# The output blocks of the last attention head, placed over all seven of its visits instead of the last six

## The reference

```
h = modulate(rms_norm(x, mix_norm), sh2, sc2)
q, f_fwd, f_bwd, i, g, rx, rgate = split(h @ w_in)
o_hg = hgrn2_mixer(q, f_fwd, f_bwd, i, g, ...)   # 4 heads x 128, chunkwise, both directions
       # per head: scores with decay between all pairs of tokens, o = scores @ v,
       # o = rms_norm(o) * silu(g)
o_rg = rglru_mixer(rx, rgate, ...)               # gated linear recurrence, 4 tiles of 128 channels
y = concat([o_hg, o_rg]) @ w_out                 # 1024 x 1024
x = x + g2 * y
```

## Time and profile before

| | us |
|---|---|
| median of 3 runs | 1004.42 |
| lowest and highest run | 1002.71, 1004.58 |
| the profiled execution, its own time | 1005.18 |
| its span in the profile | 1003.5 |
| TensorE (PE) busy in the span | 978.0 (97%) |
| VectorE (DVE) busy | 790.5 (79%) |
| ScalarE (ACT) busy | 511.7 (51%) |

### The profile page before, as it was taken

The page is one execution under the profiler, slowest core; times in us unless marked ns, Lnnn a source line. Parts: engine busy times, 40 slices in busy tenths (PEclk is TensorE's granted clock), DMA queues, the critical chain, the costliest instruction groups (busy, mean ns, idle before and its releaser), DMA issues.

```text
span 1003.5 us, 18868 instructions
## 1 busy us (share of the span) xinstructions
PE 978.0 (97%) x6956; PEld 851.7 (85%) x6956; DVE 790.5 (79%) x1052; ACT 511.7 (51%) x700; POOL 234.6 (23%) x229
## 2 busy tenths in 40 slices
PE   7999999999999999999999989999999999999997
PEld 6779999999888888686677767788999999988887
DVE  6788899988788858879999985878888999673334
ACT  6545444455333133688977963575554454433311
POOL 0025554452112301101100000402554454100100
PEclk9999999999999999999999999999999999999999
DMA  9568888884788826622222202245888787552322
GB/s 350 222 179 203 199 187 200 183 201 151 261 294 284 310 94 230 198 95 79 66 84 63 66 22 79 70 126 140 207 209 199 178 198 168 189 189 85 104 84 85
DMA packets 65622, 163.79 MB, mean 163 GB/s; under 512 B 6848, under 2 KB 9168, under 8 KB 65568
## 3 DMA queue, kind: packets, MB, share of 16 engines
q1 hardware_dynamic: 45296, 110.80, 32.9%
q0 software_dynamic: 18992, 50.16, 21.7%
q10 hardware_dynamic: 1280, 2.10, 0.9%
HBM read 158.83 MB, written 2.10 MB: 160 GB/s over the span
## 4 chain that ended last, share of the span: by engine, by line
PE 83%; DVE 7%; ACT 5%; issue 2%; DMA 1%; SPq 1%; DVEq 0%; ACTq 0%
PE psum L2030 14%; PE psum L2032 13%; PE psum L2031 13%; PE psum L2119 11%; PE psum L2121 11%; PE psum L2120 11%; DMA early<-wada 1%; PE psum L2427 1%; DVE wlo L1209 1%; ACT whi L640 1%; PE psum L2421 1%; DVE forms L1549 1%; PE psum L2351 1%; PE psum L2352 1%; PE psum L2353 1%
## 5 line engine op out<-in xcount | busy, mean ns | idle before, releaser
L1209 DVE TENSOR_TENSOR wlo<-raw,whi 128x1024 fp32r<-128x1024 f32 x94 | 119.4, 1270 | 110.9 <-ACT whi L640 110.5
L640 ACT ACTIVATE whi<-raw 128x1024 fp32r<-128x1024 f32 x92 | 97.3, 1058 | 207.0 <-PE psum L2032 193.0
L2030 PE MATMUL psum<-ghi,whi 128*128 128x512 f32 (+2 forms) x384 | 143.4, 373 | 0.0
L2031 PE MATMUL psum<-glo,whi 128*128 128x512 f32 (+2 forms) x384 | 142.6, 371 | 0.0
L2032 PE MATMUL psum<-ghi,wlo 128*128 128x512 f32 (+2 forms) x384 | 142.6, 371 | 0.0
L2030 PE MATMUL psum<-hhi,whi 128*128 128x512 f32 x304 | 122.5, 403 | 1.9 <-DVE wlo L1209 1.9
L2119 PE MATMUL psum<-forms,hi 128*128 128x256 f32 x432 | 119.2, 276 | 0.0
L2120 PE MATMUL psum<-forms,hi 128*128 128x256 f32 x432 | 119.2, 276 | 0.0
L2121 PE MATMUL psum<-forms,lo 128*128 128x256 f32 x432 | 119.2, 276 | 0.0
L2032 PE MATMUL psum<-hhi,wlo 128*128 128x512 f32 x304 | 118.7, 390 | 0.0
L2031 PE MATMUL psum<-hlo,whi 128*128 128x512 f32 x304 | 118.6, 390 | 0.0
(11 more groups left out here) (299 smaller groups left out, 2428.2 us busy)
## 6 DMA issues: line engine op xcount, KB each, us to landing
raw<-wu SPq DMA_DIRECT2D x96, 512.0 KB, 3.4
ada<-wada POOLq DMA_DIRECT2D x56, 512.0 KB, 5.0
sraw_a<-ws SPq DMA_DIRECT2D x36, 256.0 KB, 4.0
sraw_a<-ws SPq DMA_DIRECT2D x18, 512.0 KB, 4.0
sraw_b<-ws SPq DMA_DIRECT2D x36, 256.0 KB, 3.1
sraw_a<-ws POOLq DMA_DIRECT2D x36, 256.0 KB, 4.2
raw<-ws SPq DMA_DIRECT2D x36, 256.0 KB, 3.9
raw<-ws SPq DMA_DIRECT2D x18, 512.0 KB, 4.0
```

The costliest lines, as they stand in the source:

```text
L640: nc.scalar.activation(whi[:, slot, :], raw[:, slot, :], ACT.Copy).then_inc(hi_done, 1)
L1209: nc.vector.tensor_tensor(wlo[:, slot, :], raw[:, slot, :], whi[:, slot, :], ALU.subtract).then_inc(lo_done, 1)
L2030: nc.tensor.matmul(dst, a, rhi, start=start, stop=False)
L2031: nc.tensor.matmul(dst, a, rlo, start=False, stop=False)
```

## The change

Before, the first visit of the last head had no output blocks in front of it, and visits 1 to 6 had four each. After, a table gives the first block of each visit: four blocks stand in front of visits 0, 1 and 2, and three in front of visits 3 to 6. The sum is 24 both ways.

```diff
@@ -368,6 +368,8 @@
+
+        OUT_AT = (0, 4, 8, 12, 15, 18, 21, 24)
@@ -2492,8 +2494,8 @@
                 for g, steps in enumerate(STEPS_AT[r == 3]):
                     if r < 3:
                         z_half(first + g // 2, g % 2)
-                    elif g:
-                        out_blocks(4 * (g - 1), 4 * g)
+                    else:
+                        out_blocks(OUT_AT[g], OUT_AT[g + 1])
                     if (r, g) in ((1, 0), (2, 0), (3, 0)):
                         pv(r - 1)
                     for s in steps:
```

## The result

The change made the kernel slower, by more than the range allowed: 1015.07 us median of four runs (1012.29 to 1017.14), against 1003.92 for the kernel before in the same comparison (1002.71 to 1004.58). The ratio is 1.0106, with a 95% interval of 1.0085 to 1.0128. The forecast was 1011.2, the range 1009.0 to 1014.2.

The account below looks back on a forecast made before the run. PE, busy 97%, was taken as the bound, with DVE pacing the last head from score step 2. Step 2 6.9 us late left step 10 6.8 us late: 1004.42 + 6.8 = 1011.2 us, range 1009.0 to 1014.2.

Parts of the forecast that it names:

- The mechanism of the waits: Last head: PE waits 6.9 us at block 0, then 1.3, 1.1 and 1.9 us at later visits.
- the clock: Last head: half clock for 3.6 us from block 0's restart; the old half clock around step 0 gone.
- Part 1: Blocks 0 to 3 ahead of pv(2): PE idles 6.9 us for ylo of tile 0; score step 2 6.9 us late.
- Rival (d): Seam: ylo of tile 0 already there, blocks fill the gap, step 2 1.5 us early: 1002.9 us; chance 0.03.
- Part 2: Blocks 8 to 11 ahead of step 3: PE waits 1.3 us more for ylo of tile 2, covered by step 6.
- Part 3: Three blocks before visits 3 to 6: 1.9 us idle before block 16; step 10 6.7 to 6.9 us late.
- rival (b): Steps 2 to 10: DVE's chain has slack, time given back: +2.3 us, 1006.7; chance 0.10 with halfway cases.
- I take half clock at the restart and for 3.6 us: At block 0 after 6.9 us idle: 8.4 of 12 matmuls at half clock, four blocks take 4.4 us.
- Rival (a): Blocks 16 to 20: a second clock drop, 3.4 us at 1.2 GHz costing 1.7 us: +8.5, 1012.9; chance 0.28.
- rival (c): Seam: half clock through blocks 0 to 3 and pv(2), 4.1 us more: +10.9, 1015.3; chance 0.05.

Follow-up runs that it names:

- b3: The kernel before, profiled again without an edit: 1005.03 us.
- b1: The kernel before, profiled again without an edit: 1003.93 us.
- b2: The kernel before, profiled again without an edit: 1002.42 us.
- e11: The kernel before with filler matmuls, 5 in front of score step 0 of the last head and 4 before step 1: 1003.10 us against 1003.52, ratio 1.0000.
- a4: The changed kernel again, no edit, its fourth profile: 1017.09 us, run once.
- e12: The changed kernel again, no edit: 1014.79 us median of three, ratio 1.0115 to the kernel before.
- e0: The changed kernel again, no edit: 1013.48 us median of four, ratio 1.0101 to the kernel before.
- e1: The changed kernel with 28 filler matmuls in front of block 0: 1012.95 us, ratio 1.0096 to the kernel before.
- e2: As e1, with more filler matmuls: 5 before block 8, 4 before step 6, 8 before block 16: 1010.99 us, ratio 1.0066 to the kernel before.
- e6: The changed kernel with DVE's ylo of tile 0 moved ahead of far_scores(3): 1008.65 us, ratio 1.0041 to the kernel before.
- e4: The changed kernel with no blocks in visit 0 and eight in visit 1: 1009.81 us, ratio 1.0051 to the kernel before.
- e5: The changed kernel with pv(2) ahead of blocks 0 to 3 instead of behind them: 1009.91 us, ratio 1.0070 to the kernel before.
- e7: The changes of e5 and e6 joined, with block table 0, 4, 8, 12, 14, 16, 20, 24: ratio 0.9992 to the kernel before.

## Why the prediction was wrong

The mechanism of the waits held, and one term, the clock, was mis-sized in both kernels. All lengths of the head in us:

| profile | head's length | clock loss | the rest |
|---|---|---|---|
| before: first, b3 | 35.08, 35.06 | 1.7, 1.7 | 33.4, 33.4 |
| before: b1, b2, e11 | 33.50, 33.46, 33.48 | 0 | 33.5 |
| changed: first, a4 | 45.67, 45.58 | 5.9, 5.7 | 39.8, 39.8 |
| changed: e12, e0 | 43.72, 42.63 | 3.8, 2.6 | 39.9, 40.1 |
| e1, e2 | 43.33, 40.26 | 3.4, 0 | 40.0, 40.3 |
| forecast for the changed kernel | 41.8 | 1.8 | 40.0 |

The last column is the waits and the work. It differs by 6.5 us between the kernels and is the same in every profile of either to 0.3 us, or 0.5 with the filler. The forecast has it to 0.2 us.

- Part 1 was right: idle from the end of the spread to `ylo` of tile 0, 6.98 us for 6.9 forecast, with pv(2) and the score steps held back. e6 shows that this `ylo` is the releaser. Rival (d) is out by that.
- Part 2 was right: 1.3 us forecast, 1.29 measured, and covered up to step 6 by the DVE chain, whose wait there was 1.18 us. From step 2 to step 6 it is 10.95 us in the first profile, and was 10.96 before, so this stretch is DVE's, as read.
- Part 3 was right: 1.9 us forecast in front of block 16, 1.91 measured. The four blocks saved did not come back, and rival (b) is out.
- The step that failed is "I take half clock at the restart and for 3.6 us", with all that hangs on it. I took the length of the stretches in the trace of before, 3.2 and 3.6 us, for a place where PE idles three times as long, and put nothing into the sum for the clock behind block 16. In the four profiles of the changed kernel PE was busy at half clock for 5.2 to 11.8 us of the head. At the seam these are 4.2 to 6.2 us: through three blocks in one profile, all four in another, and into pv(2) in two. At block 16 they are 0, 3.4, 5.5 and 5.6 us. Rival (a), to which I gave 0.28 and a stretch of 3.4 us, so came in three of four, in two of them longer than that, and the beginning of rival (c) beside it. As alternatives, each alone, they stood inside or just outside of the range; together they are beyond it. That (c)'s 1015.3 is close to the measured 1015.07 is luck: in none of the four profiles did half clock run through pv(2).
- The same term failed on the side of before. The 1.7 us of clock loss at its seam were taken for a part of the kernel, which the change takes away. Two of four profiles of before don't have it. For the median this set off a loss that half of these profiles do not have: against b1 and b2 the changed heads are 9.1 to 12.2 us longer.
- The times of the comparison follow from it: 6.5 us of waits, plus 2.6 to 5.9 of clock loss in the changed kernel, less 0 to 1.7 in the one before, is 7.4 to 12.4, around the measured 9.2 to 11.3 of the medians of the three comparisons. In the means of the four profiles of each kernel it is 6.5 + 4.5 - 0.9, and 0.8 from behind step 10, together 10.9. e2, which has no half clock in the head, is 6.75 us above before.

What remains open is what decides in which executions the clock falls. With the same waits, to 0.02 us, it fell or did not; the runs show that it varies, not by what.

## What to carry to other kernels

A filler placed in front of a wait only helps if its own inputs are ready before that wait ends; look up the releaser of the filler's first operand and what stands behind it in the same in-order queue. Where an engine paces a chain, work moved ahead of the chain's trigger delays all of it, and work saved behind the trigger is not given back. And before a clock loss is counted for or against a change, profile the kernel more than once: a term that comes and goes in the kernel before cannot be set off against the new one, and waits of 1 to 2 us must each be priced with the half clock that may follow them.

## What the runs showed of the hardware

Half clock was not tied to a single wait's length. Waits of 1.17 and 0.96 us close together were followed by it in two profiles of the kernel before and not in two others. A wait of 1.29 us was not followed by it in four profiles of the changed kernel, nor in e4 and e5, and was in e1, e6 and e7. A wait of 2.91 us (e5, one profile) was not. Nor need the fall come inside the wait: at block 16 it came 0.8 to 1.4 us after PE had started again in e1, e4, e5, e6 and e12. A wait of 6.98 us (four profiles of the changed kernel) was followed by 4.2 to 6.2 us of work at 1.2 GHz, and the granted clock had already fallen while PE stood idle, 1.9 to 4.4 us into the wait. Short matmuls of 0.22 us in the waits kept the clock at 1.00 for the whole head (e2). The runs of the changed kernel spread over 4.9 us (1012.29 to 1017.14), those of before over 1.9 (1002.71 to 1004.58) in the same comparison. In a later one, of 29 runs of before, 28 took 1002.38 to 1005.47 us and one 1008.56.
